# Two softmax branches of an attention layer: the gate over the sum is applied to the untransposed probabilities instead of to the output

## Chip, cores and metric

One NeuronCore of a Trainium2 chip runs the kernel. The metric is the device time of one execution in microseconds (us). Engines: PE is TensorE (its matmuls; PEld its weight loads), VectorE is DVE in the rows, ScalarE is ACT, GpSimd is POOL, and SP only issues transfers.

## The reference, cut to what matters

The program computes four layers (two of one network, two of another) on a sequence of 512 rows of 1024 columns, all in float32. The change touches one of them, sparse attention with 16 heads of 64 columns. Each head has three branches, and with this length the selection takes every block and the window covers every key, so two of them are full causal softmaxes over 512 keys:

```python
p_c = _masked_softmax(s_c, d_c >= 0)            # 31 compressed keys
o_c = einsum('ghqn,ngd->qghd', p_c, vc)
p_s = _masked_softmax(s_s, m_s[:, None])        # selected keys
o_s = einsum('ghqk,gqkd->qghd', p_s, v_sel)
p_w = _masked_softmax(s_w, m_w)                 # window
o_w = einsum('ghqk,kgd->qghd', p_w, vw)
o = g[..., 0:1] * o_c + g[..., 1:2] * o_s + g[..., 2:3] * o_w
return o @ w_out
```

`_masked_softmax` divides `exp(s - max)` by its row sum, at least 1e-30. The scores carry a bias of slope times distance.

## The kernel before, in words

**Tiling.** Heads go in 8 pairs, and a pair takes two *steps*: the even step n = 2j is the selected branch of pair j, the odd step n = 2j + 1 its window branch. A step has four query tiles q = 0 to 3 of 128 rows; tile q has (q + 1) x 128 keys. The two heads of a pair (hd = 0, 1) lie in the two halves of the partitions.

**One step.** PE makes the scores of tile q for both heads (`scores`, L1853) in PSUM banks that go round three. VectorE adds the bias and takes the row maximum in one pass (`masked`, L2144); GpSimd makes the bias of a pair ahead of time, after the last `masked` of an earlier odd step (L1789 to L1791). ScalarE takes the exponential with its row sum (`exps`, L2019). PE transposes the probabilities in three groups of key tiles, g = 0 (4 blocks a head), 1 (3 blocks) and 2 (3 blocks) (`turn`, L1922), into bank 3 for hd = 0 and bank 4 for hd = 1. ScalarE copies bank 3 and VectorE bank 4 to SBUF (`take_turned`, L2062 and L2193; of group 2 ScalarE copies both). PE multiplies with the values (`values`, L1938) into bank 5 for even and 6 for odd steps.

**The small things.** On even steps PE also makes the scores against the 31 compressed keys (`scores_cmp`, L1862); VectorE masks them (`masked_cmp`, L2153 to L2159), ScalarE takes one exponential (L2088), and in the next step VectorE sums and weighs them (`weigh_cmp`, L2167 to L2175). In every step VectorE turns the row sums into gate over sum (`weigh`, L2180 to L2184); PE transposes both small things (`turn_small`, L1947), ScalarE copies them (`take_small`, L2071), PE spreads the two rows of weights over 128 partitions (`spread`, L1952), ScalarE copies that (`take_spread`, L2079), and VectorE multiplies the output with it and adds the branches up (`combine`, L2198 to L2205). The compressed branch's values product (`values_cmp`, L1957) takes a score bank. At the end of a pair ScalarE and VectorE split the sum in a high and a low part (L2100, L2225) for the output projection.

**What sets the order.** Every engine runs its own list, written out by hand, in order; semaphores link them. Step n does its own scores, and beside them the transposes and values of step n - 1 (i = 1, 2, 3) and, at i = 0, the last values group of step n - 2. PE's list in one step: `scores` 0, `spread`, `values` 2 of the step before last; `scores` 1, (`values_cmp`), `turn` 0; `scores` 2, `turn` 1, `values` 0, `turn_small`; `scores` 3, `turn` 2, `values` 1, (`scores_cmp` on even steps). After the last step the output projection (`out_part`) is woven in. No weights are loaded during the stretch.

Of the kernel before, what the change touches and what calls it, by code (L numbers as in the profile page):

```python
# [14 lines left out]
F32 = mybir.dt.float32  # L15
# [5 lines left out]
P = 128  # L21
# [20 lines left out]
def build(nc, a, out):  # L42
    ctx = ExitStack()
    with ctx:
# [1626 lines left out]
        mt_dve, mt_pe, ms_act, rr_pe = sem("mt_dve"), sem("mt_pe"), sem("ms_act"), sem("rr_pe")  # L1671
        cx_dve, cx_act, o_mul, o_sum = sem("cx_dve"), sem("cx_act"), sem("o_mul"), sem("o_sum")
        o_hi, o_lo, rs_act = sem("o_hi"), sem("o_lo"), sem("rs_act")
# [98 lines left out]
        def pool_nsa(e, stage, chain):  # L1772
            e.wait_ge(n_sum, norm_no[stage])
            chain(e.memset(tmp[:, :, :], 0.0))
            for h in range(2):
# [4 lines left out]
            chain(e.memset(pick, 1.0))  # L1780
            chain(e.affine_select(out=pick, in_=pick, compare_op=ALU.is_ge, fill=0.0, base=0, pattern=[[1, P]],
                                  channel_multiplier=-HD))
            chain(e.affine_select(out=pick, in_=pick, compare_op=ALU.is_ge, fill=0.0, base=HD - 1, pattern=[[-1, P]],
                                  channel_multiplier=HD))
# [57 lines left out]
        def pe_nsa(pe, stage):  # L1842
            def free_bank(v):
                if v >= 3:
                    pe.wait_ge(sc_dve, v - 2)

            def scores(n, q):
# [3 lines left out]
                for hd in range(2):  # L1851
                    r = slice(hd * HD, hd * HD + HD)
                    pe.matmul(pbank[unit_no[n, q, hd] % 3][:, 0:nk], qT[r, j, q * P:q * P + P], keys[r, j // 4, 0:nk],  # L1853
                              start=True, stop=True).then_inc(sc_pe, 1)

            def scores_cmp(n):
                j = n // 2
                free_bank(unit_no[n, "c", 1])
                for q in range(QT):
                    for hd in range(2):  # L1860
                        r = slice(hd * HD, hd * HD + HD)
                        ins = pe.matmul(pbank[unit_no[n, "c", hd] % 3][:, 32 * q:32 * q + NC], qT[r, j, q * P:q * P + P],  # L1862
# [1846 lines left out]
```

## Time and profile before

| what | value |
|---|---|
| median of 3 runs | 3488.65 us (3488.27 to 3488.86) |
| the profiled execution's own time | 3483.9 us |
| span in its profile | 3482.2 us |
| mean granted clock of PE | 0.993 |
| PE busy | 3398.7 us, 98% of the span |
| VectorE, ScalarE, GpSimd busy | 2411.0, 1472.3, 1065.8 us |

The attention of this layer lies between 646 and 866 us after the span's start, in slices 7 to 9 of the page's 40; the rest of the program isn't touched. A busy PE in these views need not be at its peak, since matmuls are pipelined and their ends are modelled; the distance between two starts of the same kind is the safer reading.

### The profile page before, as it was taken

The numbers are of one execution on the slowest core, as the hardware profiler recorded it, in microseconds if no ns is written. First come the engines' busy times: TensorE is split into PE (matmuls) and PEld (weight loads), VectorE is DVE, ScalarE is ACT, GpSimd is POOL, SyncE is SP. The second block draws the span as 40 slices with busy tenths as digits, with TensorE's granted clock in tenths as the row PEclk, the third lists the DMA queues.
The fourth block names the chain that finished last, engine by engine and source line by source line (L and its number), as shares of the span: only waits on it lengthen the run. The fifth ranks groups of instructions, "written<-read, shape, count | busy, mean of one in ns | idle before, by whom it ended". The sixth has DMA issues, their size and how long they took to land. (4 is left out here: it accounts for less than half of the span.)

```text
span 3482.2 us, 56148 instructions
## 1 busy us (share of the span) xinstructions
PE 3398.7 (98%) x21983; PEld 2867.9 (82%) x21983; DVE 2411.0 (69%) x3238; ACT 1472.3 (42%) x2096; POOL 1065.8 (31%) x687
## 2 busy tenths in 40 slices
PE   8999999999999999999999999999999999999998
PEld 6889988645889978997777789988998888878997
DVE  6687774466777777786567587778777534468786
ACT  5644442465444453333544343344333422244333
POOL 1243322010243235443024045524542100015452
PEclk9999999999999999999999999999999999999999
DMA  3333334100223223333200133322322222213331
GB/s 122 97 101 106 103 105 97 37 1 13 97 98 106 99 85 98 108 101 98 64 26 8 57 103 104 108 85 97 110 96 97 85 85 85 85 58 103 107 101 69
DMA packets 232580, 296.26 MB, mean 85 GB/s; under 512 B 21893, under 2 KB 201464, under 8 KB 232392
## 3 DMA queue, kind: packets, MB, share of 16 engines
q1 hardware_dynamic: 230864, 290.48, 25.6%
q0 software_dynamic: 1152, 3.05, 0.4%
q8 instruction: 131, 2.15, 0.3%
q14 instruction: 57, 0.47, 0.0%
q10 hardware_dynamic: 376, 0.12, 0.0%
HBM read 291.53 MB, written 2.10 MB: 84 GB/s over the span
## 5 line engine op out<-in xcount | busy, mean ns | idle before, releaser
L337 DVE TENSOR_TENSOR wlo<-raw,whi 128x2048 fp32r<-128x2048 f32 x266 | 660.3, 2482 | 278.2 <-ACT whi L331 249.2
L331 ACT ACTIVATE whi<-raw 128x2048 fp32r<-128x2048 f32 x178 | 340.8, 1915 | 639.7 <-PE bank L343 549.2
L341 PE MATMUL bank<-u_hi,whi 128*128 128x512 f32 x1440 | 563.3, 391 | 4.2 <-DVE arena L3498 2.4
L343 PE MATMUL bank<-u_hi,wlo 128*128 128x512 f32 x1440 | 561.5, 390 | 0.0
L342 PE MATMUL bank<-u_lo,whi 128*128 128x512 f32 x1440 | 560.9, 389 | 0.0
L341 PE MATMUL bank<-h_hi,whi 128*128 128x512 f32 (+1 forms) x1340 | 536.0, 400 | 22.2 <-DVE h_lo L1136 9.9
L343 PE MATMUL bank<-h_hi,wlo 128*128 128x512 f32 (+1 forms) x1340 | 522.1, 390 | 0.0
L342 PE MATMUL bank<-h_lo,whi 128*128 128x512 f32 (+1 forms) x1340 | 522.1, 390 | 0.0
L509 PE MATMUL bank<-th,whi 128*128 128x256 f32 x1408 | 394.5, 280 | 2.3 <-DVE tmp L745 2.3
L511 PE MATMUL bank<-th,wlo 128*128 128x256 f32 x1408 | 392.8, 279 | 0.0
L510 PE MATMUL bank<-th,whi 128*128 128x256 f32 x1408 | 392.8, 279 | 0.0
L465 ACT ACTIVATE whi<-raw 128x2048 fp32r<-128x2048 f32 x88 | 168.5, 1915 | 457.2 <-PE bank L511 208.1
L341 PEld LDWEIGHTS bank<-h_hi,whi 128*128 128x128 f32 x1340 | 253.1, 189 | 92.7 <-issue 26.0
L341 PEld LDWEIGHTS bank<-u_hi,whi 128*128 128x128 f32 x1440 | 270.7, 188 | 60.8 <-DVE arena L3498 3.6
L343 PEld LDWEIGHTS bank<-u_hi,wlo 128*128 128x128 f32 x1440 | 270.6, 188 | 58.0
L342 PEld LDWEIGHTS bank<-u_lo,whi 128*128 128x128 f32 x1440 | 270.7, 188 | 54.6 <-issue 0.2
L343 PEld LDWEIGHTS bank<-h_hi,wlo 128*128 128x128 f32 x1340 | 253.2, 189 | 53.2
L342 PEld LDWEIGHTS bank<-h_lo,whi 128*128 128x128 f32 x1340 | 253.5, 189 | 52.7 <-issue 3.6
L509 PE MATMUL bank<-th,x_hi 128*128 128x256 f32 x1056 | 295.9, 280 | 0.5
L510 PE MATMUL bank<-th,x_hi 128*128 128x256 f32 x1056 | 294.5, 279 | 0.0
L511 PE MATMUL bank<-th,x_lo 128*128 128x256 f32 x1056 | 294.5, 279 | 0.0
L509 PEld LDWEIGHTS bank<-th,whi 128*128 128x128 f32 x1408 | 264.3, 188 | 5.3 <-DVE tmp L745 3.1
(494 smaller groups left out, 6377.3 us busy)
## 6 DMA issues: line engine op xcount, KB each, us to landing
raw<-in_ffn_wgu SPq DMA_DIRECT2D x88, 1024.0 KB, 5.1
raw<-in_ffn_wd SPq DMA_DIRECT2D x44, 1024.0 KB, 4.8
raw<-in_mlp_w_up SPq DMA_DIRECT2D x32, 1024.0 KB, 5.3
raw<-in_mlp_w_down SPq DMA_DIRECT2D x32, 1024.0 KB, 4.8
raw<-in_odd_w_in SPq DMA_DIRECT2D x24, 1024.0 KB, 5.1
raw<-in_even_w_in SPq DMA_DIRECT2D x13, 1024.0 KB, 5.3
raw<-in_rg_w_in SPq DMA_DIRECT2D x8, 1024.0 KB, 5.3
raw<-in_odd_w_out SPq DMA_DIRECT2D x8, 1024.0 KB, 5.0
```

The source lines that it names most:

```text
L331: e.activation(whi[:, n % 2, :], raw[:, n % 2, :], ACT.Copy).then_inc(hi_ready, 1)
L337: e.tensor_tensor(wlo[:, n % 2, :], raw[:, n % 2, :], whi[:, n % 2, :].bitcast(F32), ALU.subtract).then_inc(lo_ready, 1)
L341: pe.matmul(o, w_hi, r_hi, start=first, stop=False)
L342: pe.matmul(o, w_hi, r_lo, start=False, stop=False)
L343: return pe.matmul(o, w_lo, r_hi, start=False, stop=last)
L465: e.activation(whi[:, n % 2, :], raw[:, n % 2, :], ACT.Copy).then_inc(hi_ready, 1)
L509: pe.matmul(pbank[half + r][:, LEFT], hi, th[:, j, t, 1, :], start=first, stop=False, skip_group_check=True)
L510: pe.matmul(pbank[half + r][:, LEFT], hi, th[:, j, t, 0, :], start=False, stop=False, skip_group_check=True)
L511: ins = pe.matmul(pbank[half + r][:, LEFT], lo, th[:, j, t, 1, :], start=False, stop=last, skip_group_check=True)
```

## The change

The weights of a tile (gate over sum) are made as soon as its exponentials are done, and each head's untransposed probabilities are multiplied by them in place: ScalarE does hd = 0 (`scale_a`), VectorE hd = 1 (`scale_b`). `turn` 0 waits for these products. All three branches of a pair then accumulate in one bank (5 or 6 by pair), and `spread`, `take_spread` and `combine` go. `turn_small` and `take_small` run once a pair, at the start of the next even step, through the bank that the next pair will take, which has to be split and free first (`o_lo`). ScalarE and VectorE split the sum from PSUM. The score banks are four, 7 included, from step 1 on. `masked_cmp` is cut in two (`shift_cmp` is its second part).

```diff
-        rr = arena[:, o:o + 8]; o += 8
+        wq = tiles(o, 2, 8); o += 16
         bias_h = (tiles(o, 2), tiles(8 * S, 2)); o += 2 * S
-        osum, oadd = arena[:, 10 * S:11 * S], arena[:, 11 * S:12 * S]
...
-        mt = tiles(o, QT, 2 * (NC + 1) + 2); o += QT * (2 * (NC + 1) + 2)
-        pick = arena[2 * (NC + 1):2 * (NC + 1) + 2, o:o + P]; o += P
+        mt = tiles(o, QT, 2 * (NC + 1)); o += QT * 2 * (NC + 1)
...
-        for n_ in range(STEPS + 1):
-            keys = [(n_, q_, hd_) for q_ in range(QT) for hd_ in range(2)] if n_ < STEPS else []
+        for n_ in range(STEPS):
+            keys = [(n_, q_, hd_) for q_ in range(QT) for hd_ in range(2)]
             if n_ % 2 == 0:
-                keys[4:4] = [(n_, "o")] if n_ else []
-                keys += [(n_, "c", 0), (n_, "c", 1)] if n_ < STEPS else []
+                keys += [(n_, "c", 0), (n_, "c", 1)]
             for key in keys:
                 unit_no[key] = len(unit_no)
+        unit_bank, bank_before, last_in = [], [], {}
+        for key, v_ in unit_no.items():
+            b_ = v_ % 3 if key[0] == 0 else (7, 0, 1, 2)[(v_ - 10) % 4]
+            unit_bank.append(b_)
+            bank_before.append(last_in.get(b_))
+            last_in[b_] = v_
...
+                for u in (v - 1, v):
+                    if bank_before[u] is not None:
+                        last = bank_before[u]
                 if v >= 3:
-                    pe.wait_ge(sc_dve, v - 2)
+                    pe.wait_ge(sc_dve, last + 1)
...
                     for k in GROUPS[g]:
                         for q in range(k, QT):
                             if g == 0:
-                                pe.wait_ge(ex_act, 8 * n + 2 * q + hd + 1)
+                                pe.wait_ge((na_scaled, nb_scaled)[hd], 4 * n + q + 1)
...
-                if g == 0 and n >= 2:
-                    pe.wait_ge(o_mul, n - 1)
+                if g == 0 and n % 2 == 0 and j:
+                    pe.wait_ge(ms_act, j)
                 for k in GROUPS[g]:
                     for hd in range(2):
                         G = 2 * (j // 4) + hd
-                        ins = pe.matmul(pbank[5 + n % 2][hd * HD:hd * HD + HD, k * P:S], v[:, k, G * HD:G * HD + HD],
-                                        probT[hd][:, K_AT[k]:K_AT[k] + (QT - k) * P], start=k == 0, stop=k == QT - 1)
+                        ins = pe.matmul(pbank[5 + j % 2][hd * HD:hd * HD + HD, k * P:S], v[:, k, G * HD:G * HD + HD],
+                                        probT[hd][:, K_AT[k]:K_AT[k] + (QT - k) * P], start=n % 2 == 0 and k == 0,
+                                        stop=n % 2 == 1 and k == QT - 1)
                 ins.then_inc(pv_pe, 1)
 
-            def turn_small(n):
-                pe.wait_ge(mt_dve, n + 1)
-                if n:
-                    pe.wait_ge(rs_act, n)
+            def turn_small(j):
+                pe.wait_ge(mt_dve, j + 1)
+                if j:
+                    pe.wait_ge(o_lo, j)
                 for q in range(QT):
-                    ins = pe.transpose(pbank[7][0:VR + 2, q * P:q * P + P], mt[:, q, :], ident[:, :])
+                    ins = pe.transpose(pbank[5 + (j + 1) % 2][0:VR, q * P:q * P + P], mt[:, q, :], ident[:, :])
                 ins.then_inc(mt_pe, 1)
...
-            def spread(n):
-                pe.wait_ge(ms_act, n + 1)
-                pe.matmul(pbank[7][:, :], pick, ms[VR:VR + 2, :], start=True, stop=True).then_inc(rr_pe, 1)
-
-            def values_cmp(n):
-                v = unit_no[n, "o"]
-                free_bank(v)
-                pe.matmul(pbank[v % 3][:, :], vcbd[:, (n // 2 - 1) // 4, :], ms[0:VR, :], start=True, stop=True)\
-                    .then_inc(sc_pe, 1)
+            def values_cmp(j):
+                pe.wait_ge(ms_act, j + 1)
+                pe.matmul(pbank[5 + j % 2][:, :], vcbd[:, j // 4, :], ms[0:VR, :], start=False, stop=False)\
+                    .then_inc(cv_pe, 1)
...
                     if n < STEPS:
                         scores(n, i)
                     if i == 0 and n >= 2:
-                        spread(n - 2)
+                        if n % 2 == 0:
+                            turn_small(n // 2 - 1)
                         values(n - 2, 2)
-                    if i == 1 and (n, "o") in unit_no:
-                        values_cmp(n)
                     if i and 1 <= n <= STEPS:
                         turn(n - 1, i - 1)
+                        if i == 2 and n % 2 == 0:
+                            values_cmp(n // 2 - 1)
                         if i >= 2:
                             values(n - 1, i - 2)
-                        if i == 2:
-                            turn_small(n - 1)
...
+            def scale_a(n, q):
+                part = prob[n % 2][0][:, Q_AT[q]:Q_AT[q] + (q + 1) * P]
+                e.wait_ge(wq_dve, 4 * n + q + 1)
+                e.activation(part, part, ACT.Copy, scale=wq[:, n % 2, 2 * q:2 * q + 1]).then_inc(na_scaled, 1)
...
+            def take_small(j):
+                e.wait_ge(mt_pe, j + 1)
+                if j:
+                    e.wait_ge(cv_pe, j)
+                e.activation(ms[0:VR, :], pbank[5 + (j + 1) % 2][0:VR, :], ACT.Copy).then_inc(ms_act, 1)
...
-                    if i == 0 and n >= 2:
-                        take_spread(n - 2)
                     if i == 0 and n % 2 and n < STEPS:
                         e.wait_ge(cx_dve, n // 2 + 1)
                         e.activation(cs[:, :, :, 0:NC], cs[:, :, :, 0:NC], ACT.Exp).then_inc(cx_act, 1)
                     if i and 1 <= n <= STEPS:
-                        if i == 3:
-                            take_small(n - 1)
                         take_turned(n - 1, i - 1, 0, pa_act)
                         if i == 3:
                             take_turned(n - 1, 2, 1, pb_act)
                             if n == STEPS:
                                 act_hi(e, n0 + 11)
+                    if n < STEPS:
+                        scale_a(n, i)
+                    if i == 0 and n % 2 == 0:
+                        take_small(n // 2 - 1)
                     if i == 2 and n >= 3 and n % 2:
                         j = (n - 3) // 2
-                        e.wait_ge(o_sum, j + 1)
-                        e.activation(rg_high(j), osum, ACT.Copy).then_inc(o_hi, 1)
+                        e.wait_ge(pv_pe, 6 * j + 6)
+                        e.activation(rg_high(j), pbank[5 + j % 2][:, :], ACT.Copy).then_inc(o_hi, 1)
...
+            def shift_cmp(n):
+                flat = cs.rearrange("p h q n -> p (h q) n")[:, :, 0:NC]
+                e.wait_ge(sc_dve, unit_no[n, "c", 1] + 1)
...
-            def weigh(n):
-                e.wait_ge(ex_act, 8 * n + 8)
-                chain(e.tensor_scalar(rr, sums[:, n % 2, :], 1e-30, None, ALU.max))
-                chain(e.reciprocal(rr, rr))
-                if n:
-                    e.wait_ge(mt_pe, n)
-                e.tensor_tensor(mt[:, :, VR:VR + 2], rr.rearrange("p (q h) -> p q h", h=2), gates_of(n, 1 + n % 2),
-                                ALU.mult).then_inc(mt_dve, 1)
+                    ins = e.tensor_tensor(mt[:, :, 32 * hd:32 * hd + NC], cs[:, hd, :, 0:NC],
+                                          cq[:, hd].unsqueeze(2).broadcast_to([P, QT, NC]), ALU.mult)
+                ins.then_inc(mt_dve, 1)
+
+            def weigh(n, q):
+                w = wq[:, n % 2, 2 * q:2 * q + 2]
+                e.wait_ge(ex_act, 8 * n + 2 * q + 2)
+                chain(e.reciprocal(w, sums[:, n % 2, 2 * q:2 * q + 2]))
+                e.scalar_tensor_tensor(w, w, 1e30, gates_of(n, 1 + n % 2)[:, q, :], ALU.min, ALU.mult).then_inc(wq_dve, 1)
+
+            def scale_b(n, q):
+                part = prob[n % 2][1][:, Q_AT[q]:Q_AT[q] + (q + 1) * P]
+                e.wait_ge(wq_dve, 4 * n + q + 1)
+                e.tensor_scalar(part, part, wq[:, n % 2, 2 * q + 1:2 * q + 2], None, ALU.mult).then_inc(nb_scaled, 1)
...
-            def combine(n):
-                e.wait_ge(rs_act, n + 1)
-                e.wait_ge(pv_pe, 3 * n + 3)
-                e.tensor_tensor((osum, oadd)[n % 2], pbank[5 + n % 2][:, :], oadd, ALU.mult).then_inc(o_mul, 1)
-                e.wait_ge(o_mul, n + 1)
-                if n % 2:
-                    e.tensor_tensor(osum, osum, oadd, ALU.add).then_inc(o_sum, 1)
-                else:
-                    v = unit_no[n + 2, "o"]
-                    e.wait_ge(sc_pe, v + 1)
-                    e.tensor_tensor(osum, osum, pbank[v % 3][:, :], ALU.add).then_inc(sc_dve, 1)
-                    e.wait_ge(sc_dve, v + 1)
...
                     if n < STEPS:
                         masked(n, i)
+                        if i == 3:
+                            scale_b(n, 2)
+                            if (n, "c", 0) in unit_no:
+                                masked_cmp(n)
+                            weigh(n, 3)
+                            scale_b(n, 3)
+                            if (n, "c", 0) in unit_no:
+                                shift_cmp(n)
                     if i in (1, 2) and 1 <= n <= STEPS:
-                        if i == 1:
-                            if n % 2:
-                                weigh_cmp(n - 1)
-                            weigh(n - 1)
+                        if i == 1 and n % 2:
+                            weigh_cmp(n - 1)
                         take_turned(n - 1, i - 1)
-                    if i == 1 and n >= 2:
-                        combine(n - 2)
-                    if i == 3:
-                        if n >= 3 and n % 2:
-                            j = (n - 3) // 2
-                            e.wait_ge(o_hi, j + 1)
-                            e.tensor_tensor(rg_low(j), osum, rg_high(j).bitcast(F32), ALU.subtract).then_inc(o_lo, 1)
-                        if (n, "c", 0) in unit_no:
-                            masked_cmp(n)
+                    if i < 3 and n < STEPS:
+                        weigh(n, i)
+                        if i < 2:
+                            scale_b(n, i)
+                    if i == 3 and n >= 3 and n % 2:
+                        j = (n - 3) // 2
+                        e.wait_ge(o_hi, j + 1)
+                        e.tensor_tensor(rg_low(j), pbank[5 + j % 2][:, :], rg_high(j).bitcast(F32), ALU.subtract)\
+                            .then_inc(o_lo, 1)
```

## Rows read from the trace of the kernel before

**Rows 1.** Windows; per engine busy us (instructions); then PEclk, DMA share, GB/s.
```profile
736.00:740.00 4.00, 4.00 (x23) 2.56 (x24) 2.31 (x15) 3.20 (x11) 0.00 (x0) 0.68 0.02 6
```

**Rows 2.** Waits between 675 and 843 us: us, times, longest.
```profile
ACT fsum L2019 <- DVE arena L2144: 62.8, 42, 3.2
```

**Rows 3.** Timeline of PE from 792.96 us, odd step 11 into even step 12.
```profile
792.96 1.13 PE L1853 MATMUL bank<-arena 64*128 64x512 f32 x4
...
796.90 1.12 PE L1952 MATMUL bank<-arena 2*128 2x512 f32 x2 [0.39 <-ACT arena L2071]
797.96 0.87 PE L1938 MATMUL bank<-tmp,arena 128*64 128x256 f32 x8
798.76 0.70 PE L1853 MATMUL bank<-arena 64*128 64x256 f32 x4
799.29 1.02 PE L1957 MATMUL bank<-arena 64*128 64x512 f32 x2
800.24 0.66 PE L1922 MATMUL bank<-ident,fsum 128*128 128x128 f32 x4
...
801.26 0.92 PE L1853 MATMUL bank<-arena 64*128 64x384 f32 x4
...
802.91 1.08 PE L1938 MATMUL bank<-tmp,arena 128*64 128x512 f32 x4
803.92 0.63 PE L1947 MATMUL bank<-ident,arena 128*66 128x128 f32 x4
```

**Rows 4.** Timeline of PE from 804.48 us, even step 12 into odd step 13.
```profile
804.48 1.13 PE L1853 MATMUL bank<-arena 64*128 64x512 f32 x4
...
807.35 1.08 PE L1862 MATMUL bank<-arena 64*128 64x31 f32 x16
...
815.25 0.55 PE L1922 MATMUL bank<-ident,fsum 128*128 128x128 f32 x3 [0.81 <-DVE tmp L2193]
...
817.30 1.13 PE L1853 MATMUL bank<-arena 64*128 64x512 f32 x4
```

**Rows 5.** Timeline of PE: last score product of two odd steps, 7 and 9.
```profile
743.51 1.13 PE L1853 MATMUL bank<-arena 64*128 64x512 f32 x4
...
768.62 1.13 PE L1853 MATMUL bank<-arena 64*128 64x512 f32 x4
```

**Rows 6.** Timeline of VectorE from 811.80 us: what runs ahead of the copy.
```profile
811.80 0.42 DVE L2144 CUSTOM_DVE_ANT_0 fsum<-bank,arena 128x256 f32<-128x256 f32 x1 [1.35 <-PE bank L1853]
...
812.50 0.41 DVE L2167 TENSOR_REDUCE arena<-arena 128x8 f32<-128x248 f32 x1
...
813.99 0.17 DVE L2180 TENSOR_SCALAR arena<-arena 128x8 f32<-128x8 f32 x1
```

**Rows 7.** Groups of VectorE by form, 646 to 866 us: busy us, mean ns.
```profile
L2144 DVE CUSTOM_DVE_ANT_0 fsum<-bank,arena 128x512 f32<-128x512 f32 x24 | 15.9, 690 | 13.5 <-PE bank L1853 13.5
```

**Rows 8.** Lines of VectorE elsewhere: duration ns min/median/max, first and last start.
```profile
L2590 DVE SCALAR_TENSOR_TENSOR arena<-arena x16: 219/219/220, 1674.6 to 1739.8; 128x1 f32<-128x1 f32 x16
...
L3168 DVE TENSOR_SCALAR tmp<-tmp,par x4: 479/480/480, 1766.4 to 1882.7; 128x512 f32<-128x512 f32 x4
```

**Rows 9.** Groups of ScalarE by form, 646 to 866 us.
```profile
L2019 ACT ACTIVATE fsum<-fsum,arena 128x512 f32<-128x512 f32 x24 | 17.2, 717 | 7.7 <-DVE arena L2144 7.7
...
L2100 ACT ACTIVATE u_hi<-arena 128x512 fp32r<-128x512 f32 x4 | 2.5, 618 | 0.0
```

**Rows 10.** Timeline of PE at the end of the stretch.
```profile
841.65 1.13 PE L1853 MATMUL bank<-arena 64*128 64x512 f32 x4
...
861.49 0.50 PE L341 MATMUL bank<-h_hi,whi 128*128 128x512 f32 x1
```

**Rows 11.** Timeline of GpSimd: two of the six pairs of bias products.
```profile
671.56 3.04 POOL L1791 TENSOR_SCALAR arena<-arena 128x512 f32<-128x512 f32 x2 [80.86 <-DVE arena L2144]
...
795.51 3.42 POOL L1791 TENSOR_SCALAR arena<-arena 128x512 f32<-128x512 f32 x2 [20.92 <-DVE arena L2144]
```

**Rows 12.** VectorE's line L1095, whole span: duration ns min/median/max.
```profile
L1095 DVE SCALAR_TENSOR_TENSOR h_lo<-x,par,h_hi x74: 737/751/1792, 17.1 to 3128.8; 128x512 fp32r<-128x512 f32 x74
```

More of the change, by code:

```diff
@@ L1670, in build @@
         pa_act, pb_dve, pb_act, pv_pe = sem("pa_act"), sem("pb_dve"), sem("pb_act"), sem("pv_pe")
-        mt_dve, mt_pe, ms_act, rr_pe = sem("mt_dve"), sem("mt_pe"), sem("ms_act"), sem("rr_pe")
-        cx_dve, cx_act, o_mul, o_sum = sem("cx_dve"), sem("cx_act"), sem("o_mul"), sem("o_sum")
-        o_hi, o_lo, rs_act = sem("o_hi"), sem("o_lo"), sem("rs_act")
+        mt_dve, mt_pe, ms_act, cv_pe = sem("mt_dve"), sem("mt_pe"), sem("ms_act"), sem("cv_pe")
+        cx_dve, cx_act = sem("cx_dve"), sem("cx_act")
+        wq_dve, na_scaled, nb_scaled = sem("wq_dve"), sem("na_scaled"), sem("nb_scaled")
+        o_hi, o_lo = sem("o_hi"), sem("o_lo")
         bias_pool = sem("bias_pool")
@@ L1779, in pool_nsa @@
             chain(e.memset(gz[:, :, NC:NC + 1], 0.0))
[L1780 to L1784, printed above, removed]
             for j in range(PAIRS):
@@ L1852, in scores @@
                     r = slice(hd * HD, hd * HD + HD)
-                    pe.matmul(pbank[unit_no[n, q, hd] % 3][:, 0:nk], qT[r, j, q * P:q * P + P], keys[r, j // 4, 0:nk],
+                    pe.matmul(pbank[unit_bank[unit_no[n, q, hd]]][:, 0:nk], qT[r, j, q * P:q * P + P], keys[r, j // 4, 0:nk],
                               start=True, stop=True).then_inc(sc_pe, 1)
@@ L1861, in scores_cmp @@
                         r = slice(hd * HD, hd * HD + HD)
-                        ins = pe.matmul(pbank[unit_no[n, "c", hd] % 3][:, 32 * q:32 * q + NC], qT[r, j, q * P:q * P + P],
+                        ins = pe.matmul(pbank[unit_bank[unit_no[n, "c", hd]]][:, 32 * q:32 * q + NC], qT[r, j, q * P:q * P + P],
                                         kcT[r, j // 4, 0:NC], start=True, stop=True)
@@ L2028, in act_nsa @@
                         exps(0, m)
+                        scale_a(0, m)
                 if 1 < c < 9:
@@ L2062, in take_turned @@
                 e.activation(probT[hd][:, c:c + nw], pbank[3 + hd][:, 0:nw], ACT.Copy).then_inc(done_, 1)
-            def take_small(n):
-                r = slice(VR * (n % 2), VR + 2)
-                e.wait_ge(mt_pe, n + 1)
-                if n:
-                    e.wait_ge(rr_pe, n)
-                if n >= 2 and n % 2 == 0:
-                    e.wait_ge(sc_pe, unit_no[n, "o"] + 1)
-                e.activation(ms[r, :], pbank[7][r, :], ACT.Copy).then_inc(ms_act, 1)
-            def take_spread(n):
-                e.wait_ge(rr_pe, n + 1)
-                if n % 2:
-                    e.wait_ge(o_mul, n)
-                elif n:
-                    e.wait_ge(o_sum, n // 2)
-                e.activation(oadd, pbank[7][:, :], ACT.Copy).then_inc(rs_act, 1)
+            def take_small(j):
[3 more added lines that the diff above has]
+                e.activation(ms[0:VR, :], pbank[5 + (j + 1) % 2][0:VR, :], ACT.Copy).then_inc(ms_act, 1)
             for n in range(1, STEPS + 2):
@@ L2143, in masked @@
                     e.wait_ge(sc_pe, v + 1)
-                    e.tensor_tensor_reduce(prob[n % 2][hd][:, Q_AT[q]:Q_AT[q] + nk], pbank[v % 3][:, 0:nk],
+                    e.tensor_tensor_reduce(prob[n % 2][hd][:, Q_AT[q]:Q_AT[q] + nk], pbank[unit_bank[v]][:, 0:nk],
                                            bias_h[n // 2 % 2][:, hd, S - nk:S], -1.0, -BIG, ALU.add, ALU.min,
@@ L2148, in masked_cmp @@
             def masked_cmp(n):
-                flat = cs.rearrange("p h q n -> p (h q) n")[:, :, 0:NC]
                 for hd in range(2):
```

9 lines of the change are left out of this document (2 added, 7 removed).

## The prediction

> **What bounds the kernel now.** PE is busy for 98% of the span (the table above), so only the stretch of the attention matters, and in it the question is whether PE issues without gaps. I read PE's timeline there, measuring from one product of 512 score columns (the last scores of a step, S3 for short) to the next. From the odd step 11 to the even step 12 it takes 804.48 - 792.96 = 11.52 us [rows 3, 4]; from the even step to the odd one 817.30 - 804.48 = 12.82 us [rows 4]. A pair costs 24.34 us. From starts that follow each other PE's own pieces are: spread 1.06, values 2 0.80, scores 1 0.53, compressed values 0.95, turn 0 1.02, scores 2 with turn 1 1.65, values 0 1.01, small turn 0.56, scores 3 1.06 [rows 3]. So PE is nearly filled in the odd-to-even half. In the even-to-odd half it stands before the second half of turn 1 until VectorE's copy is done, at 815.25 [rows 4], and VectorE got there late because the small sums (812.50 to 813.99, 1.49 us) run ahead of that copy [rows 6]. The two helpers lean on each other: ScalarE waits 62.8 us in 42 waits for VectorE's masked scores [rows 2]. The stretch is thus bounded by PE's list and, just behind it, by a chain through VectorE and ScalarE.
>
> **What is taken from PE.** Two spreads and one small turn a pair: 2 x 1.06 + 0.56 = 2.68 us. VectorE loses the combining and ScalarE two copies a step. If PE's list alone set the pace, that would all come back.
>
> **What is put on the helpers.** Prices: a weighing is a reciprocal and a product, each some 0.22 us [rows 8], 0.44 together; a scaling on VectorE of 512 columns by a column is 0.48 us [rows 8], on ScalarE a copy of 512 columns 0.62 us [rows 9]; an exponential of 512 columns 0.72 us [rows 9], of 256 columns some 0.5; a masked pass of 512 columns 0.69 us [rows 7], of which 0.62 to the next start, and of 256 columns 0.35 (two from 811.80 to 812.50) [rows 6]. By work this fits: some 17 us of each helper in a pair of 24. But each weighing waits for ScalarE's exponential of the same tile, and VectorE's list is in order, so whatever stands behind it waits too: the next masked scores, for which ScalarE in turn waits. Four such round trips a step are new. I walked both halves, with these durations, S3 of PE at 0.
>
> **Odd to even.** The weighing of tile 2 is done at 1.5, since its exponentials end at 1.06; masked scores 3 then run to 2.74. ScalarE scales tile 2 and splits the older pair's sum to 2.55, then takes two exponentials to 3.99. VectorE weighs tile 3 to 4.48, scales it to 4.9, and makes the low part of the split from PSUM, 0.69, to 5.6. Only then may the small turn start, because it writes the bank that was split. PE got to it at 3.57 (turn 2 from 1.55 after ScalarE's copy, 0.80; values 1 0.80; scores 0 0.42), so it stands 2.1 us, and behind it in PE's list stand values 2, scores 1 and turn 0. From 5.65: 0.56 + 0.80 + 0.60 + 1.02 + 0.85 (scores 2) gives 9.5. Scores 1 are there at 7.73, the first mask at 8.1, its two exponentials end at 9.2 and the copy at 9.8, so turn 1 starts there; 0.80 + 0.95 + 1.01 follow and S3 comes at 12.6. Before: 11.52. So +1.08.
>
> **Even to odd.** The compressed scores are there at 3.78; their masks end at 4.2, weighing and scaling of tile 3 at 5.1, the shift at 6.1, masked scores 0 at 6.54. ScalarE's exponentials end at 7.2, weighing and scaling of tile 0 at 7.9, masked scores 1 at 8.6, the small sums (1.49) at 10.1, the copy at 10.8. That is where the copy ended before, 815.2 - 804.48 = 10.7 [rows 4]: what left VectorE (its older weighing) is replaced by the wait. The second half of turn 1 and values 0 bring S3 to 12.26, without the small turn: -0.56.
>
> **The sum of the walk.** There are seven halves of each kind between S3 of steps 1 and 15, and the first odd one has no split to wait for (some 0.4 shorter than before): 6 x 1.08 - 0.4 - 7 x 0.56 = +2.2 us. At the start I find 0.2 less. The end, S3 of step 15 to the output projection's third part, took 861.49 - 841.65 = 19.84 us [rows 10]; walked the same way it is 19.1, since two spreads and a small turn leave it, but the wait of 2.1 comes in: -0.7. Together +1.3 us. The constants' set-up that GpSimd loses and the semaphores cost nothing: they are hidden under the projection ahead of the stretch, and without that cover they would be under 1 us. The fourth score bank gains nothing in the walk; the wait for a bank ends within 0.3 us of PE's need either way.
>
> **GpSimd.** Right after masked scores 3 of an odd step GpSimd makes the next pair's biases. Alone the two products take 3.04 us; beside a VectorE difference of two SBUF operands they take 3.42 [rows 11], so the two engines block each other. The other way about, VectorE's line L1095, which reads two SBUF tiles, takes 0.74 us at best and 1.79 at worst [rows 12]. Now the weighing of tile 3, with two SBUF inputs, and its scaling fall into these 3 us, ahead of the low part for which PE stands. Between 0 (they slip through) and 1.9 us: the weighing's product waits 0.42 for the first bias product, and the scaling then for all of the second, 1.5. I take the middle, 0.95, since rows show the block only for the first kind. It counts in the five odd steps that have both a bias and a split: +4.8 us (0 to 9.5).
>
> The Trainium skill (SBUF — State Buffer, Who interferes with whom) says more: a VectorE instruction in a two-port mode, which a scaling in SBUF can enter, and a GpSimd instruction exclude each other for the whole instruction. By that rule the full 9.5 would stand. No row of this case shows it for a scaling by a column.
>
> **The clock.** Between 736 and 740 us the granted clock averages 0.68 [rows 1]: for a part of it PE ran at 1.2 GHz instead of 2.4. That pair (S3 of step 7 to S3 of step 9) took 768.62 - 743.51 = 25.11 us with one such drop [rows 5], 0.77 more than 24.34. The clock column of this view shows four such drops in the stretch now, each after PE's sparsest part, the compressed scores and the waits by them. PE will stand in one piece for over 2 us in both halves, so there will be more; I take one a pair, eight: 4 x 0.77 = +3.1 us. Below, none more: 0. Above, one behind every such stop, 13 at up to 1.7 us (3.4 us at half speed, if nothing absorbs it) less today's 3: +19.
>
> **Sum.** 1.3 + 4.8 + 3.1 = +9.2 us against the profiled execution's own 3483.9 us, so 3493.1; the median of the runs shown is 4.75 us above that execution, so the forecast is 3488.65 + 9.2 = 3497.9, say 3498 us.
>
> **The rivals.**
> PE's list sets the pace (faster, 0.19). If the round trips are hidden and the low part of the split is done by the time PE reaches the small turn (at 3.6 us after S3 instead of 5.6; that is the point from which it decides), 2.68 us a pair come back: 7 x 2.68 = 18.8, 3470 us. For it speaks that PE's list was nearly full in the odd-to-even half; against it, that in the other half the copy and not PE's list was late already, and that the order on VectorE puts a wait before every masked pass.
> The walk alone (no change that can be told, 0.29): GpSimd's products slip through and the clock drops as often as now: +1.3, 3490 us. For it speaks that the drops have been only four in 200 us.
> The shared port in full (slower, 0.12): by the excluded overlap at its upper price, +9.5 instead of +4.8: 3503 us. For it speaks the 0.38 us by which GpSimd's products grew; against it, that the reverse was never seen for a scaling.
> The clock (slower, 0.10): a drop behind every stop, +19 in place of +3.1: 3514 us. Against it: waits of 0.8 us did not bring one in steps 12 and 13.
> That the scaling on VectorE is no faster from SBUF than from PSUM (0.69 instead of 0.48 us) is within the walk's own error; I give that half a microsecond a pair, 3.5 us in all.
>
> **The numbers.** The forecast has 0.30, with its own range 3492 to 3502; a seventh of it falls under the bound of 3495.6. A measurement of this kernel can tell about 0.2% from no change, 7 us. So: faster 0.19, within 0.33 (0.29 and 0.04), slower 0.48. The range leaves out most of the fastest case and a part of the clock's: 3479 to 3513 us.
>
> **What would show it.** Right: the group of waits of PE's small turn for VectorE's low part (the split), some 2 us each in 6 or 7 places; S3 to S3 distances of 12.6 or more from odd to even and about 12.3 from even to odd; scalings of tile 3 beside GpSimd's products that last over 0.5 us in five places; half-speed clock in more than four places. Wrong: distances under 11 in either half, or PE's timeline without gaps over 1 us: then PE's list was the bound and the time is near 3470. A scaling of tile 3 of steady 0.48 us beside GpSimd's products takes the second term away; four drops or fewer take the third.

## The result, and the profile after

| | before | after |
|---|---|---|
| median of 15 runs | 3488.78 us (3486.78 to 3494.69) | 3496.25 us (3491.82 to 3498.22) |
| the profiled execution's own time | 3483.9 us | 3498.2 us |
| span in its profile | 3482.2 us | 3496.5 us |
| mean granted clock of PE | 0.993 | 0.987 |

The ratio is 1.0021, interval 1.0014 to 1.0028: slower by 7.5 us, at the edge of what can be told; forecast were +9.2 us and 3498. The two profiled executions lie 14.3 us apart, since the one of before is 4.9 us under its median and the one of after 2.0 above; I read mechanisms from the profiles and sizes from both. Below, a *half* is the time from one S3 to the next, a *stop* a stretch in which PE stands, and a *drop* a piece in which PE ran at 1.2 GHz.

PE's timeline in the changed kernel, columns as in [rows 3]: first the half from even step 8 to odd step 9, then from odd 9 to even 10.

```profile
761.62 1.13 PE L1855 MATMUL bank<-arena 64*128 64x512 f32 x4
...
764.29 1.08 PE L1864 MATMUL bank<-arena 64*128 64x31 f32 x16
...
768.39 0.92 PE L1855 MATMUL bank<-arena 64*128 64x384 f32 x4
771.49 0.63 PE L1924 MATMUL bank<-ident,fsum 128*128 128x128 f32 x3 [2.19 <-ACT tmp L2065]
772.33 0.90 PE L1924 MATMUL bank<-ident,fsum 128*128 128x128 f32 x3 [0.21 <-DVE tmp L2190]
773.16 1.98 PE L1940 MATMUL bank<-tmp,arena 128*64 128x512 f32 x4
775.07 1.20 PE L1855 MATMUL bank<-arena 64*128 64x512 f32 x4
...
777.79 0.49 PE L1855 MATMUL bank<-arena 64*128 64x128 f32 x4
780.30 0.60 PE L1950 MATMUL bank<-ident,arena 128*64 128x128 f32 x4 [2.02 <-DVE u_lo L2217]
...
787.32 1.13 PE L1855 MATMUL bank<-arena 64*128 64x512 f32 x4
```

Both forecast stops are there: 2.19 us before turn 1, behind ScalarE's copy (VectorE's copy, which the walk named, ends 0.21 us later), and 2.02 us before the small turn, behind VectorE's low part (L2217). The small turn starts 780.30 - 775.07 = 5.2 us after S3; over the seven odd steps that have a split it was 5.2 to 6.1, where the walk said 5.65. The even-to-odd half took 13.45 us: it has a drop of the clock in it, seen in the values product of 1.98 us at 773.16, 1.08 elsewhere. The next half took 12.25. Before, they were 12.82 and 11.52 [rows 3, 4].

VectorE's timeline around that small turn:

```profile
778.58 0.17 DVE L2176 RECIPROCAL arena<-arena 128x2 f32<-128x2 f32 x1 [0.65 <-ACT tmp L2016]
778.78 0.16 DVE L2177 SCALAR_TENSOR_TENSOR arena<-arena 128x2 f32<-128x2 f32 x1
778.98 0.58 DVE L2182 TENSOR_SCALAR tmp<-tmp,arena 128x512 f32<-128x512 f32 x1
779.48 0.67 DVE L2217 TENSOR_TENSOR u_lo<-bank,u_hi 128x512 fp32r<-128x512 f32 x1
```

This is the round trip in four rows: the weighing of tile 3 stands for ScalarE's exponential, and scaling and low part stand behind it, though the low part needs neither.

The waits between 675 and 853 us in the changed kernel (us, times, longest):

```profile
ACT fsum L2016 <- DVE arena L2136: 35.8, 52, 1.8
PE bank L1924 <- ACT tmp L2065: 17.2, 13, 2.2
ACT fsum L2022 <- DVE arena L2177: 15.1, 23, 1.1
DVE arena L2176 <- ACT tmp L2016: 12.6, 20, 1.0
PE bank L1950 <- DVE u_lo L2217: 8.5, 4, 2.5
DVE arena L2176 <- ACT fsum L2016: 8.4, 15, 0.7
```

ScalarE's wait for masked scores, 62.8 us before [rows 2], is 35.8; new ones, each way between the helpers (L2022 for the weight, 15.1; L2176 for the exponential, 12.6 and 8.4), are what the weighing inside the tile adds.

The clock, over the whole stretch (windows view, columns as in [rows 1]), before and then after:

```profile
650.00:862.00 212.00, 194.31 (x1119) 101.25 (x1119) 130.51 (x459) 128.18 (x367) 19.77 (x12) 0.97 0.03 6
```

```profile
650.00:862.00 212.00, 174.62 (x1000) 89.82 (x998) 139.93 (x569) 146.78 (x403) 18.83 (x12) 0.90 0.03 6
```

A granted clock of 0.90 in place of 0.97 says that PE ran about 30 us more of the stretch at 1.2 GHz instead of 2.4 (0.07 x 212 us x 2). In the same view by tens of us, the clock is under 0.9 in four slices before and in ten after. Read in slices of 0.5 us, every drop in these profiles lasts 3.4 us, or two or three times that. Nine of the ten drops of the changed kernel begin between 0.5 us before and 2 us after the end of one of the long stops: one at 771.5, where the stop ends at 771.49. The busy time of a fixed window says little about the work, since the slower kernel gets less done in it. Between S3 of step 1 and S3 of step 15, which is the same work in every kernel, PE is busy for 158.6 us before (clock 0.97), 150.1 after (0.91), and 137.3 us in e4 below, which has the products of the changed kernel at a clock of 1.00. So about 20 us of PE's work did go, as meant, and PE's end did not come earlier.

**Where the 14.3 us of the two profiles lie**, by the starts of S3:

| piece | before | after | difference |
|---|---|---|---|
| to S3 of step 0 | 657.41 | 657.74 | +0.3 |
| S3 of step 0 to step 1 | 11.59 | 12.72 | +1.1 |
| S3 of step 1 to step 15 | 172.65 | 182.96 | +10.3 |
| S3 of step 15 to the third part of the output projection | 19.84 | 19.93 | +0.1 |
| the rest, which the change doesn't touch | 2620.7 | 2623.1 | +2.4 |

### The profile page after: what moved, and what is told of

Its sections match the earlier page's. It is cut to its first block and busy times, and to the rows that moved or that the text cites. A ratio compares the mean times of both kernels' runs of the same rounds, so it can differ in the third digit from the quotient of the medians.

```text
span 3496.5 us, 56092 instructions
## 1 busy us (share of the span) xinstructions
PE 3395.3 (97%) x21919; PEld 2868.7 (82%) x21919; DVE 2415.2 (69%) x3350; ACT 1494.0 (43%) x2136; POOL 1060.4 (30%) x684
```

## The experiments

The kernel before ran beside each group of them, with medians of 3488.44 (27 runs, for e0 to e3), 3488.08 (18, for e4 to e7) and 3488.96 us (21, for e8 to e10). Each group ran on a chip of its own, so a difference between kernels of two groups is safer by way of the kernel before. e3, e4, e5 and e10 have only 4 or 5 runs each, e6 has 7, the others 11.

**The changed kernel again (e0).** No edit.

> The changed kernel again, unedited, so that the runs beside it share its chip. Clock theory (the two halves of a pair are as long as before when nothing disturbs them, 12.19 + 12.25 us against 12.82 + 11.52, and the loss is the added pieces of half-speed clock, ten against four in the profiles): 0.1 to 0.3% above the kernel before, and the number and places of the drops differ from profile to profile. Waiting theory (each round trip between VectorE and ScalarE costs PE time of its own): the same 0.1 to 0.3%, but the distances from one last score product to the next are above those of before everywhere.

Measured: 3495.42 us (3493.93 to 3498.45), ratio 1.0022 (1.0013 to 1.0031). The profile repeats: 183.4 us from S3 of step 1 to S3 of step 15. Both theories hold in part: the even-to-odd half without a drop is 12.20 us (before 12.82), and the shortest odd-to-even half after the first, which has no split to wait for, is 12.78 (before 11.52).

**PE kept busy in its stops (e1).** PE makes scores again that it makes anyway, into the bank they go to, ahead of the two stops.

```diff
                     if n < STEPS:
+                        # scores(n, 0) x4 more if n is even, scores(n, 2) x3 more if n is odd; n > 1
+                        repeat(n, i)
                         scores(n, i)
```

> PE repeats score products whose bank is free anyway, just ahead of its two long stops: four extra scores 0 in even steps (1.7 us), three extra scores 2 in odd steps (2.6 us). The results are the same. No wait is removed. Clock theory: PE no longer stands still, the half-speed pieces of the stretch go to at most two, the odd-to-even half stays at 12.3 to 12.6 us, the even-to-odd one at 12.2 to 12.6, and the kernel is 6 to 10 us below the unedited one, so at the time of before or 2 us under it. Waiting theory: extra work cannot help; the same time as unedited, or up to 5 us more.

Measured: 3489.69 us (3483.81 to 3493.56), ratio 1.0001 (0.9992 to 1.0010). More work for PE made the kernel 5.7 us faster. The stretch in its profile:

```profile
650.00:862.00 212.00, 188.09 (x1242) 104.03 (x1241) 142.83 (x565) 148.46 (x404) 18.57 (x12) 0.98 0.02 4
```

The clock is back at 0.98 (1.00 between S3 of steps 1 and 15), and the halves are steady: 12.19 us even to odd, 12.95 odd to even (expected were 12.3 to 12.6), 174.1 from S3 of step 1 to that of step 15. Nothing but the stops' filling was changed, so the drops are a cost of their own, on top of the waits: 9 us between the two profiles (182.96 - 174.1), 5.7 by the medians. The profiled execution of e1 is 3.8 us under its median and the changed kernel's 2.0 above, so the 9 is at the high end for a typical run. The fill may cost something itself: in the changed kernel two pairs with hardly a drop took 24.7 us, in e1 a pair takes 25.1.

**GpSimd's products made small (e2), and both together (e7).** The bias products have 8 columns instead of 512 from pair 2 on, so those pairs' biases are left wrong but for 8 columns; VectorE and ScalarE do the same amount as before.

```diff
-                    ins = e.tensor_scalar(bias_h[j % 2][:, hd, :], dist, slope_of(head_of(2 * j, hd)), None, ALU.mult)
+                    w = S if j < 2 else 8
+                    ins = e.tensor_scalar(bias_h[j % 2][:, hd, 0:w], dist[:, 0:w], slope_of(head_of(2 * j, hd)), None, ALU.mult)
```

> From the third pair on GpSimd computes only the first 8 of 512 columns of the next pair's bias (the output is then wrong; it leaves out the rest of the product), so nothing of GpSimd runs beside the weighing and scaling of tile 3. Shared port theory as the prediction priced it (0.95 us in five places): 5 us below the unedited kernel. By the profile after, where the scaling of 512 columns takes 0.58 us beside GpSimd and 0.49 us alone: at most 0.5 us below, not to be told from zero.

> The filled kernel (extra score products ahead of PE's two stops) with GpSimd's bias products cut to 8 columns from the third pair on (output wrong for that reason). With the clock steady this weighs GpSimd's part alone. Port theory: 4 to 5 us under the filled kernel (3489.7), the odd-to-even half some 0.8 us shorter in five places. By the 0.1 us that the scaling grows beside GpSimd: 0.5 us, halves of 12.85 instead of 12.95, and the 4 us between the two unfilled kernels were the clock's.

Measured: e2 3491.44 us (3488.0 to 3494.08), 4.0 under e0; e7 3485.43 us (3481.64 to 3487.21), 4.3 under e1. The first difference is mostly not GpSimd's: in the profile of e2 31 us of the stretch ran at 1.2 GHz, in that of e0 41. Between the steady halves of e1 and e7 the difference can be read without any drop: even to odd 12.18 in both, odd to even 12.95 against 12.55. The last odd-to-even half of e1, where GpSimd has no product left to make, is 12.57 too. The scaling of 512 columns by VectorE, 675 to 842 us, in e1 and in e7 (busy us, mean ns):

```profile
L2195 DVE TENSOR_SCALAR tmp<-tmp,arena 128x512 f32<-128x512 f32 x6 | 4.8, 808 | 0.2
```

```profile
L2196 DVE TENSOR_SCALAR tmp<-tmp,arena 128x512 f32<-128x512 f32 x6 | 2.9, 487 | 0.2
```

Beside GpSimd's products a scaling takes 0.32 us longer on average over these six (five at 0.87, one at 0.49), and the odd-to-even half grows by 0.4; over the 14 halves 174.1 against 171.97, +2.1 us. The other 2 us between the medians of e1 and e7 are not explained. The price in the forecast was 0.95 in each of five places.

**No weighing and no scaling (e3).** `weigh`, `scale_a` and `scale_b` are left out on both engines, so the two softmax branches lack their gate over sum. Turn 0 waits for the exponentials again.

```diff
-                                pe.wait_ge((na_scaled, nb_scaled)[hd], 4 * n + q + 1)
+                                pe.wait_ge(ex_act, 8 * n + 2 * q + hd + 1)
```

> Weighings and scalings are left out on both engines (the output lacks gate over sum for two branches); everything else is as in the changed kernel. If these round trips hold PE back: no stop of 2 us is left, a pair takes 20.5 to 22 us instead of 24.4, and the kernel is at 3465 to 3475 us. If PE's list or the other waits set the pace: a pair over 23.5 us and the kernel above 3485 us.

Measured: 3454.57 us (3451.88 to 3456.19), ratio 0.9902 (0.9887 to 0.9918), 41 us under the changed kernel and 10 under the expected range, with halves of 10.82 and 10.54. What PE was relieved of does come back, and more (2.98 us a pair, where 2.68 were taken from PE), once the helpers don't have to weigh. Work and waits are taken away together here; the next experiment parts them.

**Each tile weighed one tile later (e4).** Tile q is weighed and scaled behind masked scores q + 1 (ScalarE's part behind its next exponentials), and the low part of the split stands right behind masked scores 3. All work stays.

```diff
-                    if n < STEPS:
-                        scale_a(n, i)
+                    late_n, late_q = (n, i - 1) if i else (n - 1, 3)
+                    if late_n < STEPS:
+                        scale_a(late_n, late_q)
...
                         masked(n, i)
+                        # low part of the split here, at i == 3 of odd steps from 3 on
+                    late_n, late_q = (n, i - 1) if i else (n - 1, 3)
+                    if 0 <= late_n < STEPS:
+                        weigh(late_n, late_q)
+                        scale_b(late_n, late_q)
```

> The change with another order: each tile is weighed and scaled one tile later (tile 3 after the next step's masked scores 0), so that its exponentials are done when VectorE comes to it, and the low part of the split stands right behind masked scores 3. Same instructions, same banks. If the round trips behind each masked pass are what holds the changed kernel back: an even-to-odd half of some 11.5 us (12.2 unedited), an odd-to-even half of some 10.7 (12.9 in the filled kernel), few drops of the clock, 3472 us. If the work put on VectorE and ScalarE itself is the bound: halves as in the unedited kernel and 3495 us.

Measured: 3469.89 us (3466.78 to 3471.05), ratio 0.9945 (0.9932 to 0.9958): 18.2 us under the kernel before. PE in it, from S3 of an even step on:

```profile
769.71 1.13 PE L1855 MATMUL bank<-arena 64*128 64x512 f32 x4
...
777.15 0.77 PE L1924 MATMUL bank<-ident,fsum 128*128 128x128 f32 x5 [1.15 <-ACT fsum L2022]
...
779.70 0.55 PE L1924 MATMUL bank<-ident,fsum 128*128 128x128 f32 x3 [0.46 <-DVE tmp L2192]
...
781.19 1.13 PE L1855 MATMUL bank<-arena 64*128 64x512 f32 x4
```

The even-to-odd half is 11.48 us with no stop over 1.2, the other 10.91; there is one drop in the whole stretch, at its start. The same instructions in another order are worth some 25 us: it was the waits of the two helpers for each other, with the drops that they bring, not their work. A pair is 24.34 - 22.39 = 1.95 us shorter than before, of the 2.68 that PE was relieved of; the rest of the 18.2 us comes from drops that the kernel before has (2.3 us in its profile between S3 of steps 1 and 15) and from outside these halves.

**The copy of turn 0 ahead of the small sums, in e4 (e5) and in the kernel before (e6).** On VectorE:

```diff
+                        take_turned(n - 1, i - 1)
                         if i == 1 and n % 2:
                             weigh_cmp(n - 1)
-                        take_turned(n - 1, i - 1)
```

> As the one before, and VectorE's copy of turn 0 runs ahead of the compressed branch's small sums. If that copy is what PE waits for in the even-to-odd half: 10.9 us there in place of 11.5, 3467 us. If not, the same as the one before.

> The kernel before, with only VectorE's copy of turn 0 ahead of the small sums and the weighing. If the copy was late there as read from the trace: the even-to-odd half goes from 12.82 to some 11.7 us, 3481 us. If another wait stands right behind it (ScalarE's copies): 12.6 us and 3487.

In e6 the copy passes the weighing too, which the kernel before does there in every step.

Measured: e5 3467.22 us (3466.61 to 3468.72), ratio 0.9941 (0.9928 to 0.9954); e6 3497.63 us (3494.03 to 3507.68), ratio 1.0033 (1.0020 to 1.0046), a miss by 17 us and of sign. In e5 the median was right for a wrong reason: the even-to-odd half fell to 10.80, but the other grew to 11.60, and the pair stayed at 22.4. In e6 VectorE's copies of turn 0 in even step 12 and odd step 13 read:

```profile
810.76 0.69 DVE L2193 COPY tmp<-bank 128x512 f32<-128x512 f32 x1 [1.11 <-PE bank L1922]
...
822.75 0.69 DVE L2193 COPY tmp<-bank 128x512 f32<-128x512 f32 x1 [0.25 <-PE bank L1922]
```

And PE, at turn 2 of step 11 and in the half from step 12 to step 13:

```profile
803.88 0.87 PE L1922 MATMUL bank<-ident,fsum 128*128 128x128 f32 x6 [0.58 <-ACT tmp L2062]
...
813.95 1.13 PE L1853 MATMUL bank<-arena 64*128 64x512 f32 x4
...
823.82 0.87 PE L1922 MATMUL bank<-ident,fsum 128*128 128x128 f32 x6 [0.26 <-ACT tmp L2062]
...
827.31 1.13 PE L1853 MATMUL bank<-arena 64*128 64x512 f32 x4 [1.05 <-DVE arena L2144]
```

The stop at turn 1 (0.81 us before [rows 4]) is gone, as meant: the whole turn waits 0.26. But the copy now stands for PE's turn, 1.11 us in the even step, a gap that the weighing had partly filled, and 0.25 in the odd one. The sums and the weighing come after it, masked scores 2 are later, and S3 stands 1.05 us for the score bank that they free. A pair without a drop costs 11.79 + 13.36 = 25.15 us against 24.34, and the stretch has 31 us at 1.2 GHz instead of 14. So the copy's lateness before [rows 4, 6] was no free gain: another wait stood right behind it, and it was not ScalarE's copies, which the second expectation named.

**The low part first, alone (e8).** The changed kernel with one instruction moved:

```diff
                         if i == 3:
+                            # the low part of the split, odd steps from 3 on (was behind shift_cmp and scale_b)
                             scale_b(n, 2)
```

> The changed kernel with one move: VectorE makes the low part of the split right behind masked scores 3, ahead of the weighing of tile 3; all else keeps its place. Round trips through the small turn (theory 1): the low part ends about 3.5 us after PE's S3 instead of 5.6, the small turn no longer stands for 2 us, scores 1 come 2 us earlier, and ScalarE's copy is then late at about 8.7 instead of 9.8: the odd-to-even half falls from the 12.95 us that it takes without clock drops to about 11.5 to 11.8, six halves, 3495.4 - 7 to - 9 = 3487 to 3489 us; if the stops that are left bring fewer drops of the clock, down to 3484. Theory 2, the chain of the weighings through both helpers sets the half and the small turn's stop only hides it: turn 1 waits longer by what the small turn gives back, the half stays at 12.7 or more, and the time stays within 2 us of 3495. The even-to-odd half stays at 12.2 by both.

Measured: 3479.04 us (3475.21 to 3484.73), ratio 0.9976 (0.9967 to 0.9985), 16.4 us under e0 (16.9 by way of the kernel before), twice what I expected. VectorE and PE after it:

```profile
791.54 0.69 DVE L2202 TENSOR_TENSOR h_lo<-bank,h_hi 128x512 fp32r<-128x512 f32 x1
792.15 0.41 DVE L2182 TENSOR_SCALAR tmp<-tmp,arena 128x384 f32<-128x384 f32 x1
```

```profile
789.16 1.13 PE L1855 MATMUL bank<-arena 64*128 64x512 f32 x4
...
792.38 0.60 PE L1950 MATMUL bank<-ident,arena 128*64 128x128 f32 x4
793.47 0.87 PE L1940 MATMUL bank<-tmp,arena 128*64 128x256 f32 x8 [0.49 <-ACT tmp L2065]
...
797.53 0.55 PE L1924 MATMUL bank<-ident,fsum 128*128 128x128 f32 x3 [0.69 <-ACT tmp L2065]
```

The small turn starts 3.2 us after S3 (3.2 to 4.4 in all steps) and waits for nothing, but for 0.30 us in the last one. The odd-to-even half is 11.9 us instead of 12.95 (six halves, 6.4 us), and the even-to-odd half keeps its 12.2 and its stop of 2.18, as theory 1 said. The rest I put down to the clock: with one of the two long stops gone, four drops are left in the stretch in place of ten, and its granted clock is 0.97. Theory 2, that the stop would only move to turn 1, fell: turn 1 waits 0.69.

**The kernel before with PE kept busy (e9).** Two repeats of scores 0 in odd steps.

```diff
                     if n < STEPS:
+                        repeat(n, i)     # scores(n, 0) twice more, odd n from 3 on
                         scores(n, i)
```

> The kernel before with PE kept busy: in odd steps from step 3 on it makes scores 0 two times more into a bank that it is about to fill anyway (0.84 us of PE, same results), which falls into the stops behind the compressed scores and at the second half of turn 1. If the kernel before also pays for its own drops of the clock (theory 1: 0.77 us each, four in the stretch), they go and the time is 3488 - 3 = 3485 us, with pairs of 24.3 to 24.6 us from S3 to S3 throughout; then the change must be weighed against 3485 and not against 3488, and its schedule alone costs 3489.7 - 3485 = 4 to 5 us. If the drops are no price for the kernel before, or the extra products are not hidden (theory 2: 0.84 us in each of seven halves, less the 1.4 us of stops that they can fill), it stays at 3488 or goes to 3490 or more.

Measured: 3491.18 us (3487.29 to 3492.99), ratio 1.0006 (0.9997 to 1.0015). This is theory 2, the extra products not hidden: the even-to-odd half grew from 12.82 to 13.27 us and the drops did not go (31 us of the stretch at 1.2 GHz, 14 before), so this fill kept no clock up. What the kernel before pays for its own drops is not settled by it. Its own profile shows three between S3 of steps 1 and 15, and the halves that have them are 1.25, 0.23 and 0.77 us [rows 5] longer than 12.82: 2.25 in all, 0.75 on average.

**Three score banks in e4 (e10).** 

```diff
-            b_ = v_ % 3 if key[0] == 0 else (7, 0, 1, 2)[(v_ - 10) % 4]
+            b_ = v_ % 3
```

> The kernel in which each tile is weighed one tile later (3469.9 us), with three score banks in turn instead of four; the bank that is freed stays empty. If the fourth bank gains nothing, as the prediction has it, 3470 us within 2 us, and halves of 10.9 and 11.5. If PE's scores run further ahead of VectorE in this version and need the fourth bank, scores wait for a bank that VectorE frees: halves longer by 0.3 to 0.8 us each, 3475 to 3482 us.

Measured: 3466.26 us (3464.75 to 3467.79, 5 runs), ratio 0.9935 (0.9921 to 0.9948), halves of 10.92 and 11.48 as with four. In this order of the work the fourth bank gains nothing; the 3.6 us by which this median is lower lie outside the halves (one drop of 3.4 us at the start of the stretch instead of 6.8), and I don't ascribe them to the bank. This and e5 are the fastest kernels of the study that do all the work, 0.6% under the kernel before.

## Why the prediction was right

**PE's list.** 2.68 us of work a pair were to leave PE and not to come back. So it was: some 20 us of PE's work went and the kernel became slower, and the rival that its list sets the pace needed a small turn at 3.6 us after S3; it started at 5.2 to 6.1. e4 shows that the rival describes the same work without the round trips: 18.2 us faster, where the rival was priced at 18.8. That the two figures lie so close is chance in part, since e4 gives back 1.95 of the 2.68 us a pair and gets the rest elsewhere.

**The walk.** Both stops were there in place and size: 2.02 us forecast at 2.1, 2.19 forecast as over 2. The small turn stood in six places in the rows above, 11.7 us in all (8.5 for `u_lo`, 3.2 for `h_lo`), and in a seventh, 1.57, at the end. For the stretch between S3 of steps 1 and 15 the walk gave +2.2 us. Without drops and with GpSimd's products small (e7) it took 171.97 us; before, without its three drops in that piece, 7 x 24.34 = 170.4: +1.6. By halves too the walk was near e7: 12.26 for the even-to-odd half, measured 12.18; 12.6 for the other, measured 12.55. In the changed kernel itself the odd-to-even halves with hardly a drop took 12.25 and 12.49 us, a little under the 12.6 named as a sign of being right. The -0.7 us at the end did not come (+0.1, a drop lies there), nor the -0.2 at the start (+0.3).

**GpSimd.** Right in place and sign, but far too large: forecast +4.8 us. The mis-sized step is "I take the middle, 0.95". Of the two parts of that price, the weighing's product, for which 0.42 us of waiting were put down, took 0.16 to 0.17 us in every one of its places in the changed kernel. The scaling waited for no whole product: in the five odd steps with both a bias and a split it took 0.58, 0.88, 0.59, 0.58 and 0.59 us against 0.49 alone, 0.8 us longer in all. The first and second of them:

```profile
700.23 0.58 DVE L2182 TENSOR_SCALAR tmp<-tmp,arena 128x512 f32<-128x512 f32 x1
...
725.05 0.88 DVE L2182 TENSOR_SCALAR tmp<-tmp,arena 128x512 f32<-128x512 f32 x1
```

How much it grows went by where it falls: the four short ones start 1.3 us after GpSimd's pair of products, the long one, like all five of e1 (0.87 to 0.88), 1.7 us after it. So the 2.1 us between e1 and e7 are the price in e1, and an upper bound for the changed kernel; its two pairs with hardly a drop took 24.68 and 24.74 us, no more than e7's 24.73 with small products. For the scaling of the step above, 0.58 us at 778.98, the products began at 777.69:

```profile
777.69 3.21 POOL L1790 TENSOR_SCALAR arena<-arena 128x512 f32<-128x512 f32 x2 [23.74 <-DVE arena L2136]
```

The Trainium skill (SBUF — State Buffer, Who interferes with whom) has a VectorE instruction in a two-port mode, which a scaling in SBUF can enter, and a GpSimd instruction exclude each other for a whole instruction; by that rule the 9.5 us at the top of the range would stand. The trace does not bear out a wait of a whole product here: 0.88 us was the longest scaling of the changed kernel and of e1, against 0.49 alone.

The wait of the weighing's product that the forecast had is real in another order: in e4, where it falls elsewhere beside GpSimd's products, it took 0.60 to 0.62 us in three of its 64 places.

```profile
740.74 0.62 DVE L2179 SCALAR_TENSOR_TENSOR arena<-arena 128x2 f32<-128x2 f32 x1
```

**The clock.** The mechanism was right and this term too small in the profiles. Forecast: eight drops instead of four, +3.1 us. Measured: ten places, of which one lasts twice and one three times 3.4 us, so thirteen such pieces instead of four. In the profiles, S3 of step 1 to that of step 15 has 182.96 - 174.1 = 8.9 us by drops after and 172.65 - 170.4 = 2.3 before, so +6.6, and most of the +1.1 of the first half besides; by the medians e1 takes back 5.7, of which before has its 2.3, so about 3.4, near the forecast. The step that was short is "I take one a pair": with two long stops in a pair a pair often had two. The price of 0.77 us a drop was read from one pair [rows 5]; the three drops of that kernel cost 1.25, 0.23 and 0.77, and that their mean, 0.75, is the price of the one chosen is luck.

**The sum.** In the stretch: walk +1.6 (2.2), GpSimd +2.1 (4.8), clock +6.6 (3.1), together the 10.3 of the table; the forecast of the three is 10.1. The three measured terms are steps from before by way of e7 and e1 to the changed kernel, so they add up by construction, and the borders between them are less sure than the sum: with the 0.8 us for GpSimd that the changed kernel itself shows, the clock's share would be about 7.9. A term that was too large and one that was too small offset each other, so the hit of the sum is partly luck: the median of 3496.25 is 1.7 us under the forecast. What none of the terms had is how much hung on one instruction: the rival "walk alone" took the order on VectorE as given.

## What to carry to other kernels

When a step moves from the output to the tiles, ask on both in-order engines what stands behind each new wait that does not need it: moving one such instruction (e8) was worth 16 us, and that move together with weighing one tile later (e4) 25 us, with no work taken away. A stop of the matmul engine has a second price where the granted clock falls after it, so two moderate stops can cost more than their lengths. Before moving a late instruction to the front, look at what it will wait for: other work may have been filling that gap, and what it overtakes becomes late in its turn (e6).

## What had not been expected of the hardware

- More products for PE made the kernel 5.7 us faster (e1), by the clock alone: 0.98 instead of 0.90 over 212 us. The same means with fewer products did not help the kernel before (e9): the time did not change clear of noise, and more of the stretch ran at 1.2 GHz (31 us instead of 14).
- GpSimd's products slowed an in-place scaling of 512 columns on VectorE by an amount that went by its start: 0.49 us alone, 0.58 when it began 1.3 us after GpSimd's pair of products, 0.87 when it began 1.7 us after (e1 and the changed kernel). The weighing's product, two SBUF operands of 2 columns, took 0.16 to 0.17 us in all 64 places of e1 and of the changed kernel, but 0.60 to 0.62 us in three of the 64 of e4.
- No stop of PE in the changed kernel's stretch was over 2.5 us, and nine of its ten drops of the clock begin about where such a stop ends.
